# A fused two-block kernel: the second block's mixer with every product in three terms

## The reference

```
hc = modulate(rmsnorm_2(ctx, g_mix_pre), csh1, csc1)           # 256 context rows
kv_c = hc @ w_in[:, OFF_K:OFF_G]                               # K and V of the context
h = modulate(rmsnorm_2(x, g_mix_pre), sh1, sc1)
proj = h @ w_in                                                # 1024 x 5120
y_hy = hyena_branch(proj[..., :OFF_Q]) @ w_hy_up               # 512 -> 1024
q, k = rope_2d(...), rope_2d(...);  v = proj[..., OFF_V:OFF_G]
o = diff_attention(q, [k, k_c], [v, v_c], lam)                 # softmax 1 - lam * softmax 2
y_att = heads_out(o, subln_g, lam_init) @ w_att_up             # 512 -> 1024
g_hy, g_att = split(sigmoid(proj[..., OFF_G:]))
mixed = (g_hy * y_hy + g_att * y_att) @ w_out
x = x + g1 * rmsnorm_2(mixed, g_mix_post)
x = x + g2 * rmsnorm_2(swiglu(modulate(rmsnorm_2(x), sh2, sc2)), g_ffn_post)
```

## Time and profile before

| what | us |
|---|---|
| median of 3 runs | 1460.58 |
| the profiled execution's own time | 1458.51 |
| its span, first to last instruction | 1456.8 |
| PE busy in the span | 1354.2 |
| DVE busy | 650.5 |
| ACT busy | 415.7 |

### The profile page before, as it was taken

One profiled execution on the slowest core, in us unless ns is written; L12 is line 12 of the kernel. 1 busy time (PEld: TensorE's weight loads), 2 busy tenths in 40 slices (PEclk: granted clock), 3 DMA queues, 4 the chain that ended last, 5 costly groups with the idle time before them and its releaser, 6 DMA issues.

```text
span 1456.8 us, 18061 instructions
## 1 busy us (share of the span) xinstructions
PE 1354.2 (93%) x6984; PEld 886.5 (61%) x6984; DVE 650.5 (45%) x1166; ACT 415.7 (29%) x645; POOL 28.6 (2%) x61
## 2 busy tenths in 40 slices
PE   5999998999999999999999999889998889699998
PEld 5978876955645444444544454349844344699976
DVE  4785667532435222222222222246754543555544
ACT  5356564321122211111111111234201231344433
POOL 2000202000000000000000000000000000000000
PEclk9999999999999999999999999999999999799999
DMA  9443538939644899999999999924405133355420
GB/s 344 180 174 116 208 130 294 321 116 336 237 164 174 343 428 427 429 428 428 428 428 428 429 428 429 402 74 145 174 0 187 58 116 104 119 182 174 174 87 29
DMA packets 100109, 359.66 MB, mean 247 GB/s; under 512 B 3938, under 2 KB 29798, under 8 KB 87697
## 3 DMA queue, kind: packets, MB, share of 16 engines
q1 hardware_dynamic: 96928, 349.77, 61.5%
q0 software_dynamic: 3120, 9.05, 1.9%
HBM read 357.76 MB, written 1.05 MB: 246 GB/s over the span
## 4 chain that ended last, share of the span: by engine, by line
PE 65%; DMA 22%; DVE 7%; ACT 3%; issue 2%; SPq 1%; DVEq 0%; ACTq 0%
PE bank L452 27%; DMA ring<-in_w 20%; PE bank L490 12%; PE bank L806 8%; PE bank L1033 4%; PE bank L499 2%; PE bank L824 1%; DMA ring<-in_w_xkv 1%; PE bank L734 1%; PE bank L916 1%; PE bank L926 1%; DMA ring<-in_w_in 1%; ACT ring_parts L1761 1%; PE bank L782 1%; DVE ring_parts L1080 1%
## 5 line engine op out<-in xcount | busy, mean ns | idle before, releaser
L1080 DVE TENSOR_TENSOR ring_parts<-ring,ring_parts 128x1024 fp32r<-128x1024 f32 x170 | 205.5, 1224 | 182.1 <-ACT ring_parts L1761 175.3
L452 PE MATMUL bank<-arena_parts,ring_parts 128*128 128x256 f32 x1920 | 238.7, 288 | 16.5 <-DVE ring_parts L1080 6.1
L452 PEld LDWEIGHTS bank<-arena_parts,ring_parts 128*128 128x128 f32 x1920 | 237.8, 197 | 17.4 <-issue 17.3
L1761 ACT ACTIVATE ring_parts<-ring 128x1024 fp32r<-128x1024 f32 x170 | 177.8, 1057 | 244.7 <-PE bank L452 209.0
L806 PE MATMUL bank<-ring,arena 128*64 128x512 f32 x512 | 226.1, 594 | 12.6 <-DMA ring<-in_w 11.9
L807 PE MATMUL bank<-ring,arena 128*64 128x512 f32 x512 | 226.5, 595 | 0.0
L452 PE MATMUL bank<-ring_parts,arena_parts 128*128 128x512 f32 x816 | 191.2, 395 | 10.2 <-DVE ring_parts L1080 6.5
L452 PEld LDWEIGHTS bank<-ring_parts,arena_parts 128*128 128x128 f32 x816 | 154.4, 191 | 44.6 <-issue 8.2
L806 PEld LDWEIGHTS bank<-ring,arena 128*64 128x64 f32 x512 | 67.6, 137 | 153.7 <-issue 153.7
L490 PE MATMUL bank<-ring,arena 128*128 128x512 f32 x320 | 142.7, 605 | 8.6 <-issue 4.1
L824 PE MATMUL bank<-ring,arena 128*64 128x512 f32 x512 | 113.4, 595 | 1.1 <-DMA ring<-in_w 1.1
(11 more groups left out here) (363 smaller groups left out, 1196.7 us busy)
## 6 DMA issues: line engine op xcount, KB each, us to landing
ring<-in_w SPq DMA_DIRECT2D x96, 2048.0 KB, 16.9
ring<-in_w_in SPq DMA_DIRECT2D x26, 2048.0 KB, 8.9
ring<-in_w_ada SPq DMA_DIRECT2D x12, 2048.0 KB, 8.0
ring<-in_w_ffn_gate SPq DMA_DIRECT2D x11, 1024.0 KB, 5.1
ring<-in_w_ffn_up SPq DMA_DIRECT2D x11, 1024.0 KB, 7.7
ring<-in_w_ffn_down SPq DMA_DIRECT2D x5, 2048.0 KB, 7.8
ring<-in_w_xkv SPq DMA_DIRECT2D x4, 2048.0 KB, 22.3
ring<-in_w_out SPq DMA_DIRECT2D x4, 2048.0 KB, 13.7
```

The lines of the kernel that those rows point to most:

```text
L452: mm = pe.matmul(ps[:, o:o + width], *pair, start=(o == 0 and k == 0 and ha + hw == 0), stop=(k == KD - 1 and ha == 1), skip_group_check=True)
L1080: dve.tensor_tensor(low, src, high, ALU.subtract).then_inc(low_ready, 1)
L1761: act.activation(high, src, ACT.Copy).then_inc(high_ready, 1)
```

## The change

1. Context K and V get units of their own, p4x and p5x (the same columns, loaded a second time), and the context activations are split in the first expert step (`ctx_parts`), so these products are in three terms too. So are the gates, hyup, attup, mo0 and mo1.
2. The split main activations lie in a ring slot (`hT`), so 4 slots are left for weights. When the gates are done, that slot gives 4 further places for high parts: 8 in all.
3. The order of products is p4x, turn, p5x, p0, p1, p2, p4. The units p3, p5 and p6 to p9 are cut in quarters (`filler`) and put between the transforms, the transposes and the attention steps.
4. In attention the transposed weights of step n are multiplied by V one step later (`attended(n - 1)`), the buffers are double, the copy of the transposed weights moves from DVE to ACT, and DVE forms p1 + mixing * p2 in one instruction and scales the result by 1/sum as it leaves its bank.
5. attup, mo0 and mo1 go half by half of the tokens, so that the sum of the first half is turned while the second is multiplied; mo0's and mo1's split parts stay for the second half. The normed first half is turned inside mo1.
6. In the feed-forward part PE no longer waits for all `up` banks before the down products, quarters are split up to 8 ahead, and the last four chunks are done bank by bank.

```
-            AT.append(i % R)
+        if i < N_BEFORE:
+            AT.append(i % R)
+        elif name == "hT":
+            AT.append((N_BEFORE + R - 1) % R)
+        else:
+            AT.append((N_BEFORE + turns[0] % (R - 1)) % R)
...
+            high_places = deque(4 * R + q for q in range(4))
...
+            def quarter_ready(name, q):
+                n = len(SPLIT)
+                place = high_places.popleft()
+                high_places.append(place)
+                SPLIT.append((name, q, place, last_in[place]))
+                last_in[place] = n
+                pe.wait_ge(high_ready, n + 1)
+                pe.wait_ge(low_ready, n + 1)
...
+            def split_quarter(name, q, acts, jobs, kn=KD, banks=None):
+                if q == 0:
+                    for n, (job, _) in enumerate(jobs):
+                        take(job, None if banks is None else banks[n])
+                quarter_ready(name, q)
+                wts = weights(name, q, kn)
+                for job, places in jobs:
+                    mm = three_terms(PS[JOB[job][0]], places, q, acts, wts, kn)
...
-            for nm in ("p4", "p5"):
-                token_major(f"{nm}c", hcT, unit(nm, KD, 512), KD)
...
+            split_tokens("p4c", "p4x", ctx_parts)
+            turn([f"hT{i}" for i in range(4)], hatH, hats=10)
+            split_tokens("p5c", "p5x", ctx_parts)
...
+            filler("p3", 0, 1)
+            transformed(0)
+            filler("p3", 2, 3)
+            convolved(0)
+            filler("p5", 0)
+            transformed(1)
+            filler("p5", 1, 2, 3)
+            convolved(1)
+            filler("p6", 0, 1)
...
             for n in range(H * NT):
                 if n + 1 < H * NT:
                     dscores(n + 1)
-                gate_half(n)
-                pe.wait_ge(s["a_ready"], n + 1)
...
+                filler(("p7", "p8")[n // 4], n % 4)
+                turned_weights(n)
+                if n:
+                    attended(n - 1)
+            filler("p9", 0)
+            attended(H * NT - 1)
+            filler("p9", 1, 2, 3)
...
-            emptied(pe, *jobs_of("up", FC // 2))
...
@@ vector
-            split_low()
-            turned_modulated([f"hT{i}" for i in range(4)], actT, 0, 0, 0)
-            split_activations(mixer2_parts)
-            split_low()
+            split_low(2)
+            for n in range(4):
+                turned_modulated([f"hT{i}" for i in range(4)], hT_plain, 0, 0, 0, (n,))
+                if n:
+                    split_activations(hT_parts, hT_plain, (n - 1,))
+            split_activations(hT_parts, hT_plain, (3,))
+            split_low(6)
...
+            filtered(0)
+            split_low(1)
+            gated_on(0)
+            split_low(3)
+            emptied(dve, "p3_0", "p3_1")
+            rotate(Q)
+            filtered(1)
+            split_low(2)
+            gated_on(1)
...
+            for n in range(H * NT):
+                if n + 1 < H * NT:
+                    maxima(n + 1)
+                split_low(1)
+                if n + 1 < H * NT:
+                    differ(n + 1)
+                if n:
+                    attended(n - 1)
...
@@ scalar
+                if n + 1 < H * NT:
+                    exponentials(n + 1)
+                split_high(1)
...
+                did(act.activation(aT[:, n % 2], ps[:].rearrange("p (k n) -> p k n", k=4), ACT.Copy), free(f"aT{n}"), hold=False)
```

More of the change, by code:

```diff
@@ L12 @@
+from collections import deque
 from contextlib import ExitStack
@@ L110, in weight_units @@
     w2 = w["w_in_2"][0]
-    for j in (4, 5, 0, 1, 2, 3):
+    for name, j in (("p4x", 4), ("p5x", 5), ("p0", 0), ("p1", 1)):
+        whole(name, cols(w2, 512 * j))
+    add("hT")
+    for j in (2, 4):
         whole(f"p{j}", cols(w2, 512 * j))
     tables("dftB")
-    for j in range(6, 10):
+    for j in (3, 5, 6, 7, 8, 9):
         whole(f"p{j}", cols(w2, 512 * j))
@@ L973, in _, with attended @@
+            def attended(n):
+                emptied(pe, f"aT{n}")
+                ps = take(f"do{n}", 5)
+                for j in range(4):
+                    mm = pe.matmul(ps[:, 0:DV], aT[:, n % 2, j, :], Vall[:, j, n // NT * DV:(n // NT + 1) * DV], start=(j == 0), stop=(j == 3))
+                give(f"do{n}", mm)
             dscores(0)
             for n in range(H * NT):
-                h, t = divmod(n, NT)
                 if n + 1 < H * NT:
                     dscores(n + 1)
-                gate_half(n)
@@ L994, in _, with wide_jobs @@
+            def wide_jobs(tag):
+                return [(f"{tag}{half}_{t}", [(0, 512, t, 512 * half)]) for t in range(NT) for half in range(2)]
+            emptied(pe, "zT0", "zT1")
+            pe.wait_ge(act_low, 22)
+            split_product("hyup", zT_parts, wide_jobs("hyo"), 4)
             pe.wait_ge(s["On_ready"], 8)
@@ L1012, in _ @@
-            turn([f"fT{i}" for i in range(4)], hat1, hats=12)
-            emptied(pe, *jobs_of("fT", 4))
-            pe.wait_ge(act_low, 20)
+            pe.wait_ge(act_low, 24)
+            wide = wide_jobs("atto")
+            for job, _ in wide:
+                take(job)
+            for q in range(4):
+                quarter_ready("attup", q)
+                for job, places in wide[0:2]:
+                    mm = three_terms(PS[JOB[job][0]], places, q, oT_parts, weights("attup", q, 4), 4)
+                    if q == 3:
+                        give(job, mm)
@@ new lines, in _ @@
+            for job, places in wide[2:4]:
+                for q in range(4):
+                    mm = three_terms(PS[JOB[job][0]], places, q, oT_parts, weights("attup", q, 4), 4)
+                    if job == wide[3][0]:
+                        if q == 3:
+                            give(job, mm)
+                        quarter_read("attup", q, mm, q == 3)
+                if job == wide[2][0]:
+                    give(job, mm)
+                    pe.wait_ge(s["comb2_ready"], 2)
+                    turn([f"c2T{i}" for i in range(4)], comb2, tiles_of=(0,))
@@ L1015, in _ @@
+            mixed_out(0)
+            mixed_out(1)
+            turn([f"fT{i}" for i in range(4)], hat1, hats=12, tiles_of=(1,))
+            pe.wait_ge(act_low, 32)
             for j in range(FC // 2):
@@ L1972, in step @@
                 sil(n, 1)
+                if not after and before:
+                    full(act, "logits")
+                    split_activations([f"ctxT{i}" for i in range(4)], ctx_parts, hcT)
                 high(n, 0)
@@ new lines, in _ @@
+            for t in range(NT):
+                ps = full(act, f"qT{t}")
+                did(act.activation(qT4[:, :, t * P:(t + 1) * P], ps[:].rearrange("p (h n) -> p h n", h=H), ACT.Copy), free(f"qT{t}"), hold=False)
+            split_high(2)
+            full(act, "kT3")
+            for t in range(4):
+                ps = full(act, f"kT{t}")
+                did(act.activation(kT4[:, :, t * P:(t + 1) * P], ps[:].rearrange("p (h n) -> p h n", h=H), ACT.Copy), free(f"kT{t}"), hold=False)
@@ new lines, in _, with exponentials @@
+            gate_columns(0)
+            def exponentials(n):
+                o = 8 + 8 * (n % 2)
+                act.wait_ge(s["dmax"], n + 1)
+                if n >= 2:
+                    full(act, f"aT{n - 2}")
+                for i in range(2):
+                    nm = f"ds{n}{i}"
+                    ps = full(act, nm)
+                    did(act.activation(P12[:, n % 2, i, :], ps[:], ACT.Exp, scale=0.125, bias=stat[:, o + 2 + i:o + 3 + i],
+                                       accum_out=stat[:, o + 4 + i:o + 5 + i]), s["dexp"])
+                    act.sem_inc(free(nm)[0], 1)
```

544 lines of the change are left out of this document (302 added, 242 removed).

## The result

The changed kernel took 1425.72 us (median of 4 runs, 1424.76 to 1427.03) against 1459.81 for the kernel before: a ratio of 0.977, interval 0.9759 to 0.9781. It is faster by 34 us; 42.8 were forecast, and the time lies inside the range (1401 to 1438) and inside the likeliest case's own (1407 to 1428). The profiled execution took 1424.76 us with a span of 1423.1, so the spans differ by 33.7.

What follows compares the result with a forecast made beforehand. PE's work was taken as the main bound, with chains over DVE and ACT ending last in some stretches. Mixer terms summed to 276.4 against 312.5 us, feed-forward 6.7 less: 42.8 in all, forecast 1417.5, range 1401 to 1438.

Steps and rivals of the forecast that it cites:

- the likeliest case: The whole kernel at the forecast 1417.5 us, own range 1407 to 1428; chance 0.60, with the nearby three-terms-slower case included.
- Price of a product: PE's mixer products: a 512-column unit takes 13.9 us whole, 10.85 in three terms; ten units save 30.5 us.
- Transforms: Mixer transforms, 4 x 6.9 us, with fillers p3, p5, p6: 68.5 us, one 1.4 us wait at the second back transform.
- The rival of late splits between the chains: Low parts late in DVE's list at six places, 2.3 us idle plus 1.8 slow clock each: 1441 us; chance 0.18.
- Attention: Attention steps take 5.5 us each; eight and a 2.8 us lead-in make 46.8 against 63.78 (49.5 at the table's cuts).
- the rival of the clock: Breaks in attention hold PE at the lower clock: 22 us more, 1440 us; chance 0.06.
- Head: Mixer start to p0: 30.4 us, with a 3.7 us wait before p5x's third quarter and 1.8 of slow clock.
- a sign of being right: p0 starts at 970 to 974 us, with a wait near 4 us before p5x's third quarter.
- Waits in the output part: Around hyup, attup and mo: 2.8 us for O's split, 2.7 for the turned sum, slow clock 3.6, bounds 0 to 12.
- End and feed-forward: Last mo product to gu0: 17.0 us against 15.38; feed-forward 6.7 us less, as the hole before the down products goes.
- Slower: Fillers split on demand, about 2.5 us extra for each of 40 quarters from p3 to attup: 1518 us; chance 0.04.
- named as a sign: PE stands idle 15 to 18 us before gu0 if the forecast is right.

Runs made afterwards that it cites:

- experiment 1: Changed kernel with hyup's four jobs on banks 0 to 3 instead of 3 to 6: 1416.41 us, ratio 0.9702 to the kernel before.
- experiment 8: Changed kernel with the eight gate quarters in attention (p7, p8) multiplied as whole float32 matmuls: 1428.66 us, ratio 0.979 to the kernel before.
- Experiment 6: Changed kernel with the transposed weights of step n multiplied by V in step n, not one step later: 1442.19 us, ratio 0.9896 to the kernel before.
- experiment 3: Changed kernel with both hyup on banks 0 to 3 and attup taking its second token half's banks later: 1413.01 us, ratio 0.9684 to the kernel before.
- experiment 2: Changed kernel with attup taking the banks of its second token half only when it comes to them: 1422.08 us, ratio 0.9741 to the kernel before.
- experiment 9: Changed kernel with hyup's and attup's bank edits, p5x's quarters split ahead of the activations, and the end chain's four quarters moved into its gaps: 1403.22 us, ratio 0.9616.
- Experiment 7: Changed kernel with PE waiting for all up banks again ahead of the down products: 1431.88 us, ratio 0.9817 to the kernel before.
- experiment 5: Changed kernel with the four gu0 and gu1 quarters in the end chain split in its gaps instead: 1421.60 us, ratio 0.9747 to the kernel before.

## Why the prediction was right, and where it was off

*Price of a product*: right. 10.85 us for a unit came out at 11.04 with its drain (experiment 1's hyup), and experiment 8 shows the difference of the two forms in place (0.68 us a quarter, 0.73 forecast). The 215.7 ns between matmuls of the Trainium skill (TensorE: Matmul & The Clock Gate, "Wait — 56ns, not 53.3ns?"; the formula under Back-to-back issue gap gives the same to 0.2 ns), by which the ten units would have saved an estimated 5 us more, is not seen: hyup's 48 matmuls in experiment 1 last 11.04 us with their drain, and the next work starts 10.89 us after them, so 227 ns each.

*Transforms*: right, 68.4 against 68.5, with the one wait of 1.1 us at the second back transform that was named (1.4, though its own terms, 16.7 less 15.0, make 1.7). The rival of late splits between the chains is out: DVE was busy 49.6 of 68.4 us there, and PE waited for no low part in it. Its price, 1.8 us for each idle spell over some 2.5, has the waits of 2.41 and 3.74 us behind it; the experiments show no such limit (a wait of 1.67 us with slow work behind it, one of 2.60 without).

*Attention*: right, 48.0 against 49.5, a step 5.34 against 5.5. Experiment 6 shows what the step ahead is worth in the changed kernel, 16.5 us. It does not split the gain over the kernel before, where DVE did the copy and PE waited 0.85 us for it, not 0.7 to 4.2 for ACT's. There was one wait of 1.16 us more for a quarter's low part in the second step, and 0.64 for the gates' bank. The clock was granted at 1.00, so the rival of the clock is out for this kernel; experiment 6 shows it at work where the waits are left in, for 4.3 us.

*Head*: the mechanism was right (the wait before p5x's third quarter, 3.66 us against 3.7 forecast), the size 2.6 us short. p4x's first quarter ran at the lower clock throughout (5.3 us, granted 0.50): the unit took 13.6 us (942.86 to 956.44), not 12.6, and the slow part behind the 3.66 us wait fell into p5x and not into p0, which is why the second row of the table is 1.8 us better. p0 came at 974.62, just past the 970 to 974 that was named as a sign of being right.

*Waits in the output part*: this is the term that was mis-sized. It had 5.5 us of waits here (2.8 for O's split, 2.7 for the turned sum) and 3.6 of slow clock. Measured: 6.6 before hyup, 6.1 before attup, none for the turned sum; hyup 2.5 us and attup 2.3 us slow. With 0.3 us for the normed half, that is 8.7 of the stretch's 10.3 us too many; the rest is the drain ahead of each wait and the 8 transposes of the normed half, which the forecast had in the end. The step asked only when data would be ready and found that about right: experiments 2 and 9 show O's split at 2.0 us and the turned sum at 1.9. It did not ask which of the 8 banks each job takes, so a wait for a bank is not among its terms at all. Before the change the rotation gave the last jobs' banks to those that came eight jobs later. Now the fillers take 6 and 7 by name and attention 0 to 5, so the rotation goes on at 3 and meets bank 6 with the gates still in it. That is 12.7 us by the medians, 13.3 in the trace (experiment 3).

The terms that it did have were somewhat too large, and this hid part of the miss. Without the bank waits the fifth stretch takes 60.5 us (experiment 3, 1137.04 to 1197.59) where 63.6 were forecast. By the banks alone the forecast would have been off by 3 us more; that it was not is luck. The range had room for the miss, with 0 to 12 us for the waits here, but for late data and not for banks.

*End and feed-forward*: right, 16.9 against 17.0, and 6.9 less against 6.7. Experiment 7 puts 6.2 of that on the wait that was dropped. The end's four quarters cost 4.1 us by experiment 5, where 4.9 were counted. PE stood idle 14.8 us ahead of gu0 (11.45 + 3.35), just under the 15 to 18 named as a sign.

*Slower*: out. 8.6 us is all that PE waited for low parts in the mixer, 1.16 of it between p3 and p9. Its size was wrong too: p3 to attup are 32 quarters, not 40, so 80 us and 1498.

So of the 42.8 us forecast, 2.6 less 1.8 were lost in the head, 10.3 in the output part, and 1.5 came back in attention; the other rows of the table add up to 0.4 back.

## What to carry to other kernels

When work is moved between chains, list the buffers that each job takes beside the data that it needs: a bank named for one use and left out of the rotation of the others can stand under a product that has nothing to do with it. Other banks for one product gave 9.3 us here. To put the copy that frees the bank ahead of the slow steps of ACT's list should do the same, but no run tried it. And price a wait with what follows it: in the changed kernel the waits of 3.66 to 6.58 us ahead of split products cost 1.7 to 2.7 us more at half clock. That extra counts only where PE ends last; behind the 2.02 us wait of experiment 3 it cost nothing.

## What the runs showed of the hardware

- Half clock set in not with the end of a wait but some time behind it: after the 3.66 us wait in the head, the third quarter's first matmuls ran at full rate, and the slow ones (0.63 us for one in place of 0.39) began 1.5 us later, at 968.94. The granted clock was 0.99 from 967.47 to 968.94 and 0.50 from there to 972.34.
- A wait of 1.67 us was followed by slow matmuls in experiment 6 (1133.61, scores in 1.88 us), while one of 2.60 us in the same run (1125.26) was not. Behind the same wait of 2.02 us ahead of attup, with the same products, the clock was 0.83 in experiment 3 (36 matmuls in 10.07 us) and 1.00 in experiments 2 and 9 (8.50 and 8.46). So the length of the last wait alone does not tell it; the runs show no more than that.
- Three-term matmuls with both operands in the ring ran at the same rate as with the activations elsewhere: 36 in 8.47 us at 1136.47, and 36 of attup in 8.50 in experiment 2.
